# Attention inside a two-layer trunk: mask added by VectorE, transposes two steps behind the scores, a third probability buffer, ScalarE's copy ahead of its exponential

## The reference, cut to what matters

```python
sc = einsum(qb, kc) * scale          # 31 compressed keys
pc = _masked_softmax(sc, cmp_end <= t)
o_c = einsum(pc, vc)
ss = einsum(qb, ks) * scale          # selected blocks of keys
ps = _masked_softmax(ss, tok <= t)
o_s = einsum(ps, vs)
sw = einsum(qb, kw) * scale          # window of keys
pw = _masked_softmax(sw, mw)
out = gb[0] * o_c + gb[1] * o_s + gb[2] * o_w
```

## Time and profile before

| what | value |
|---|---|
| median of 3 runs | 2489.19 us (2485.69 to 2492.6) |
| the profiled execution's own time | 2496.24 us |
| its span, first to last instruction | 2494.1 us |
| mean granted TensorE clock | 0.983 |
| busy: PE, PEld, DVE, ACT, POOL | 2335.1, 1875.6, 1435.8, 576.9, 1333.2 us |
| the twelve heads | 234 to 355, 454 to 572, 1438 to 1547 and 1644 to 1754 us |

### The profile page before, as it was taken

How to read it: one execution, slowest core, us unless ns; L and a number is a source line. 1 busy time by engine, 2 the same in 40 slices (tenths; PEclk the granted TensorE clock), 3 DMA queues, 4 the chain that set the end, 5 groups by cost and what they waited for, 6 DMA issues and landing times.

```text
span 2494.1 us, 36305 instructions
## 1 busy us (share of the span) xinstructions
PE 2335.1 (94%) x12736; PEld 1875.6 (75%) x12736; DVE 1435.8 (58%) x2460; ACT 576.9 (23%) x1114; POOL 1333.2 (53%) x1018
## 2 busy tenths in 40 slices
PE   0798999999999999999998999999999999999996
PEld 0566787877788877777886788787778888787885
DVE  8965654665677775675126155246677776335536
ACT  0211310222233333222024022022232232333001
POOL 6574447544444445555655644654544444554763
PEclk9998999998999999999999999999999999999998
DMA  9855336521122223454315533532222222221532
GB/s 351 307 210 193 121 135 230 172 102 61 67 69 68 72 73 110 155 202 156 100 63 195 197 99 103 184 121 94 69 69 71 73 69 68 69 82 62 193 135 93
DMA packets 94593, 315.92 MB, mean 127 GB/s; under 512 B 10918, under 2 KB 11174, under 8 KB 93382
## 3 DMA queue, kind: packets, MB, share of 16 engines
q1 hardware_dynamic: 86768, 295.46, 34.5%
q10 hardware_dynamic: 7644, 18.16, 2.1%
HBM read 303.86 MB, written 8.39 MB: 125 GB/s over the span
## 4 chain that ended last, share of the span: by engine, by line
PE 70%; DVE 15%; ACT 4%; POOLq 3%; issue 3%; DMA 2%; POOL 2%; DVEq 1%; ACTq 1%; SPq 0%
PE bank L653 14%; PE bank L655 14%; PE bank L654 13%; DVE arena L1715 9%; PE bank L1177 4%; PE bank L1176 4%; PE bank L1175 4%; DVE acc L1715 3%; ACT arena L1205 2%; PE bank L963 2%; PE bank L934 1%; PE bank L617 1%; POOLq L1657 1%; POOL w_lo L1655 1%; DVE tiny L1715 1%
## 5 line engine op out<-in xcount | busy, mean ns | idle before, releaser
L1655 POOL TENSOR_TENSOR w_lo<-ring,w_hi 128x512 fp32r<-128x512 f32 (+1 forms) x632 | 894.5, 1436 | 48.5 <-issue 1.3
L1651 POOL CAST w_hi<-ring 128x1024 fp32r<-128x1024 f32 (+1 forms) x320 | 356.4, 1114 | 1029.9 <-PE bank L655 844.6
L653 PE MATMUL bank<-h_hi,w_hi 128*128 128x512 f32 x1952 | 818.2, 419 | 9.3 <-POOLq L1657 9.3
L655 PE MATMUL bank<-h_hi,w_lo 128*128 128x512 f32 x1952 | 768.3, 394 | 0.0
L654 PE MATMUL bank<-h_lo,w_hi 128*128 128x512 f32 x1952 | 765.5, 392 | 0.0
L653 PEld LDWEIGHTS bank<-h_hi,w_hi 128*128 128x128 f32 x1952 | 370.9, 190 | 91.8 <-issue 15.0
L655 PEld LDWEIGHTS bank<-h_hi,w_lo 128*128 128x128 f32 x1952 | 368.8, 189 | 82.7
L654 PEld LDWEIGHTS bank<-h_lo,w_hi 128*128 128x128 f32 x1952 | 371.0, 190 | 72.5 <-issue 7.2
L1205 ACT ACTIVATE arena<-bank 128x512 f32<-128x512 f32 (+5 forms) x324 | 155.4, 480 | 660.0 <-PE bank L655 217.1
L1715 DVE SCALAR_TENSOR_TENSOR acc<-yT,cact,acc 128x1024 f32<-128x1024 f32 (+1 forms) x144 | 213.2, 1480 | 38.7 <-DMA acc<-in_b_mod 14.7
L1175 PE MATMUL bank<-w_hi,h_hi 128*128 128x512 f32 x448 | 175.7, 392 | 0.8 <-issue 0.8
(11 more groups left out here) (232 smaller groups left out, 2848.0 us busy)
## 6 DMA issues: line engine op xcount, KB each, us to landing
ring<-in_stream SPq DMA_DIRECT2D x352, 512.0 KB, 3.4
yT<-in_stream SPq DMA_DIRECT2D x128, 512.0 KB, 4.6
yT<-in_mod SPq DMA_DIRECT2D x32, 1024.0 KB, 7.8
arena<-in_x ACTq DMA_DIRECT2D x4, 1024.0 KB, 10.3
x_norm<-arena ACTq DMA_DIRECT2D x4, 1024.0 KB, 8.2
arena<-x_norm ACTq DMA_DIRECT2D x4, 1024.0 KB, 10.9
out<-arena SPq DMA_DIRECT2D x3, 1024.0 KB, 3.9
arena<-in_x SPq DMA_DIRECT2D x1, 2048.0 KB, 14.5
```

The lines of the kernel that those rows point to most:

```text
L653: mm(PJ[b][:, :], hi, h_hi[:, k, :], start=(k == 0), stop=False)
L655: last = mm(PJ[b][:, :], lo, h_hi[:, k, :], start=False, stop=(k == KT - 1))
L1651: pool.tensor_copy(w_hi[:, par, 0:w], ring[:, slot, 0:w])
L1655: pool.tensor_tensor(w_lo[:, par, at], ring[:, slot, at], w_hi[:, par, at].bitcast(F32), ALU.subtract)
```

## The change

The mask matmul goes; DVE adds the same 128x128 mask to the last block of the scores in PSUM ahead of its minimum. The transposes of a unit come one step later on PE, and so do the products with the values: a head has 12 steps, the 32 k-tiles are spread as 4, 4, 3, 3, 3, 3, 2, 2, 2, 2, 2, 2. A third probability tile `A(14)` is used. On ACT the copy of the transposed probabilities of unit s - 3 now stands ahead of the exponential of unit s - 1 in its step. The tile `mask_r` and the two conversions that fill it at the start go.

```diff
-        mask_r = sb("mask_r", [P, 2, P], F32R)
-        prob, probT = [A(0), A(1)], [A(2), A(3)]
+        prob, probT = [A(0), A(1), A(14)], [A(2), A(3)]
-        NSA_STEPS = 11
-        nsa_fill = [4, 4, 3, 3, 3, 3, 2, 2, 3, 3, 2]
+        NSA_STEPS = 12
+        nsa_fill = [4, 4, 3, 3, 3, 3, 2, 2, 2, 2, 2, 2]
...
# PE
-                                mm(SB_[(u + 1) % 2][:, 0:w], q[:, w - P:w], keys[:, 0:w], start=True, stop=False)
-                                mm(SB_[(u + 1) % 2][:, w - P:w], mask_r[:, 0, :], mask_r[:, 1, :],
-                                   start=False, stop=True).then_inc(S("scores"), 1)
+                                mm(SB_[(u + 1) % 2][:, 0:w], q[:, w - P:w], keys[:, 0:w],
+                                   start=True, stop=True).then_inc(S("scores"), 1)
-                            if 2 <= s <= 9:
-                                u = s - 2
+                            if 3 <= s <= 10:
+                                u = s - 3
...
-                                              prob[u % 2][:, j * P:(j + 1) * P], ident)
+                                              prob[u % 3][:, j * P:(j + 1) * P], ident)
-                            if 3 <= s <= 10:
-                                u = s - 3
+                            if 4 <= s <= 11:
+                                u = s - 4
...
# ACT (the exponential of unit s - 1 now follows this block)
+                            if 3 <= s <= 10:
+                                u = s - 3
+                                w = (u % TT + 1) * P
+                                act.wait_ge(S("pt_done"), H * 8 + u + 1)
+                                act.wait_ge(S("pv_done"), after("pv_done", H * 8 + max(u - 1, 0)))
+                                fn(probT[u % 2][:, 0:w], TB[(u + 1) % 2][:, 0:w], ACT.Copy)\
+                                    .then_inc(S("pt_ready"), 1)
...
# DVE
-            cp(mask_r[:, 0, :], ident)
-            cp(mask_r[:, 1, :], C("causal"))
...
                                 dve.wait_ge(S("scores"), H * 8 + u + 1)
+                                tt(b[:, w - P:w], b[:, w - P:w], C("causal"), Ad)
                                 reduce(tiny[:, u:u + 1], b[:, 0:w], AX, ALU.min).then_inc(S("max_ready"), 1)
```

More of the change, by code:

```diff
@@ L1417, in group @@
                                     .then_inc(S("pt_ready"), 1)
+                            if 1 <= s <= 8:
+                                u = s - 1
+                                w = (u % TT + 1) * P
+                                act.wait_ge(S("max_ready"), H * 8 + u + 1)
+                                fn(prob[u % 3][:, 0:w], SB_[(u + 1) % 2][:, 0:w], ACT.Exp, scale=-1.0,
+                                   bias=tiny[:, u:u + 1], accum_out=tiny[:, 8 + u:9 + u]).then_inc(S("exp_done"), 1)
                             if g == KVH - 1 and r == GROUP - 1 and s == 9:
@@ L1921, in group @@
                                 reciprocal(tiny[:, 31:32], tiny[:, 8 + u:9 + u])
-                                ts(prob[u % 2][:, 0:w], prob[u % 2][:, 0:w], tiny[:, 31:32],
+                                ts(prob[u % 3][:, 0:w], prob[u % 3][:, 0:w], tiny[:, 31:32],
                                    gate_g[:, i, 3 * r + 1 + u // TT:3 * r + 2 + u // TT], M, M).then_inc(S("probs"), 1)
```

## The result

| | before | changed |
|---|---|---|
| median | 2490.35 us (4 runs, 2485.69 to 2492.6) | 2506.11 us (4 runs, 2503.72 to 2509.18) |
| ratio, 95% interval | | 1.0065, 1.0052 to 1.0079 |
| span of the profiled execution | 2494.1 us | 2504.7 us |
| from the first matmul of head 0 to the end | 2260.3 us | 2274.0 us |

The change makes the kernel slower by 15.8 us where +6.4 was forecast: the way was right, the time lies near the upper end of the range, and the size was too small. The two profiled executions differ by less, 10.6 us in span: the one of the kernel before took 2496.24 us, 5.9 more than the median, the changed one 2506.65, 0.5 more than its own. In the second, head 0 also began 3.2 us earlier, in a stage that the change does not touch; from there on they differ by 13.8 us.

A forecast was written before the change was run, and what follows sets the result against it. PE bounds the light heads, DVE's chain the heavy ones. Losses of 9.4 us less gains of 3.0 give +6.4 on the median of 2489.19: 2495.6 us, with 8 in 10 between 2483 and 2508.

The forecast's parts named there:

- PE's bound in light heads: In heads 6 to 10 PE sets the pace; without the mask matmul, 0.067 us each, head 7 takes 35.6 us.
- The mask on DVE: A new DVE instruction ahead of each minimum, 96 in all, at 0.38 us each, 3.0 us per head.
- The work from the last transposes to the next head: PE work in a fixed order up to the next head's first matmul: 3.4 us, before and after alike.
- The place: PE's waits for scaled probabilities all stand at units 6 and 7 of heads 0 to 5 and 11, over 12 us.
- The wide bound of the mask: Upper bound of DVE's mask instruction, 0.72 us each, from sums with both inputs in SBUF.
- the sum, head by head: DVE's lateness at unit 7 from masks less filled waits: heads 0 to 5 and 11 lose 9.4 us, light heads gain 3.0.
- mask dear: Rival, 12%: on DVE's chain in all heads, 0.72 us per mask or late exponentials; +20 us, 2510 us.
- the light heads: Heads 6 to 10: 7, 8 and 10 gain 0.5 us each, 6 and 9 0.75 each, 3.0 in all.
- PE's waits for units 0 to 5 go altogether: Transposes a step later end PE's waits for these units' probabilities; waits become fewer than 14 but longer.
- ACT's order taken as 0: ACT's copy ahead of the exponential hides behind DVE and costs 0; up to 0.58 us per unit if not.
- DVE keeps up: Rival, 10%: at unit 7 of heads 1 to 5 DVE has room for the masks; faster by 15.6 us, 2473.6 us.
- The wash: Rival, 18%: pieces behind the units meet POOL less, winning 1 us in each of six heavy heads; 2489.5 us.

## Why the prediction was right in its way and short in its size

**Right.** PE's bound in light heads: 35.63 us for head 7 without POOL's split against 35.6 forecast, so the mask matmul is worth (36.18 - 35.63) / 8 = 0.069 us where 0.067 was taken (36.18 is head 7 with the mask on PE). The mask on DVE: 0.30 + 0.07 us for 0.38. The work from the last transposes to the next head: 313.42 - 310.01 = 3.41 us for 3.4. The place: 17.0 of PE's 22.2 us of waiting stand at units 6 and 7 of heads 0 to 5 and 11, where over 12 were forecast, because the masks find no room on DVE. The wide bound of the mask, 0.72, never came: the mask's mean is 300 ns with POOL's splits and without. On this the trace agrees with the rule that the prediction cites. But the Trainium skill (SBUF — State Buffer, § Who interferes with whom) makes an exception of the modes that use both ports, which the prediction left out, and the scalings, whose only tensor input is in SBUF, did get longer beside POOL.

**Mis-sized: the sum, head by head.** It took DVE's chain of before and moved it by the masks, with each instruction as long as it was, less the waits for scores that the masks would fill. The heavy heads lost 15.6 us for 9.4. The largest misses by the added waits are head 0, put at nothing because DVE had room there (PE waits 2.0 us more), and head 4, put at +0.6 (2.1 us more). The rows had scalings of one width with very different lengths, and I treated that as a property of the heads. It is a meeting with POOL, and its amount depends on when DVE arrives: the scalings of head 0 took 4.3 us before and 5.9 after, those of head 4 4.9 and 5.8 (3.6 undisturbed). In head 0 the account closes: behind unit 0 DVE waited 1.14 + 0.29 + 1.17 = 2.6 us for scores before and not at all after, seven masks of 0.37 us take the same 2.6, and the 1.6 us by which the scalings grew are what is left, against the 1.8 us of the change in that head. In head 4, 3.0 us of masks, less the 2.2 us of waits that they filled, plus 1.1 us of longer scalings and extra pieces, give 1.9 of 2.3. So the term that was too small is the stretch beside POOL, taken as unchanged; over all heads the scalings grew by 5.5 us. This is an account from the two profiles and not an experiment, and it explains only what lies above the forecast. A loss of this size does not need the growth: the mask alone on DVE costs 15 us without it, and where no scaling is stretched the mask still costs 18.3. What the runs do show is that POOL's splits as a whole make the difference between +13.8 us and about -1.5, both from head 0 to the end (2249.8 against 2251.4 us). The rival "mask dear" named POOL, but for the mask alone, which it does not touch.

**Mis-sized: the light heads, -1.4 us for -3.0.** Head 7 loses its 0.5 us again in two short waits of PE, for the compressed probabilities (0.3) and at the last transposes (0.2); both are gone without POOL's split.

**Wrong: "PE's waits for units 0 to 5 go altogether", and fewer but longer ones.** There are 24, not under 14, and 8 of them stand at units 3 and 4 (4.6 us). In head 1 they stand at units 4, 6 and 7. Unit 4, one block wide, is where the stretched scaling fell. That the range held the result while the waits were more than forecast owes something to its width.

**Wrong in part: ACT's order taken as 0.** As an edit on the changed kernel it is worth 14.9 us, and 11.5 with the mask on PE. It did no harm, as forecast, but the forecast did not see that the later transposes stand on it.

**The rivals.** "DVE keeps up" had the rows on DVE's room against it and did not come. The wash assumed that POOL is met less often; by the scalings it was met for longer.

## What to carry to other kernels

Work that is moved off the busiest engine can be dearer where it lands, when the engine that gets it stands in a serial chain with another: look for that engine's idle time ahead of the step, not for its busy share over the kernel. An instruction whose length varies in the profile at one width is meeting somebody, and a forecast that shifts it in time must ask whom it meets next. Where a consumer is put a step later, the copies in between must not stay queued behind the producer's newest step.

## What the runs showed of the hardware that was not expected

An identical scaling on DVE, 128x128 from SBUF, takes 0.346 us alone. In the changed kernel it takes 0.345 to 1.346 us; the longest run beside one of POOL's sums, the one of 1.20 beside a cast, and each ends 0.08 to 0.09 us after the piece of POOL. Of the 96 scalings 38 are more than 0.04 us longer than undisturbed ones of their width, and all 38 ran beside a POOL instruction. Reading PSUM instead, a scaling of 128x128 takes 0.410 with POOL at work. Leaving out POOL's splits in the heads, which PE never waited for there, makes the kernel before 6.5 us faster, the one with the mask on PE 10.4, and the changed one 24.2.
